# Gates issued among the tiles of a recurrent mixer's projection, a reordered beginning, and bias additions dealt out differently

## The reference, cut to what matters

```python
mod = (silu(c) @ w_ada + b_ada)                  # 6 x 1024 modulation values, from 12 panels of w_ada
h = rmsnorm(x, g_norm_mix) * (1 + sc1) + sh1
c_q, c_kv, k_pe, dil, gates = split(h @ w_in)    # projection
o_a = mla_attention(...)                         # 8 heads
o_g = dilated_band_attention(..., rel_bias, window, dilation)   # 3 groups x 8 heads
# scores there get a bias: bias_table[t5_bucket(rel)], 32 buckets, -1e30 outside the band
x = x + gt1 * ((g_a * o_a + g_b * o_b) @ w_out)
x = x + gt2 * expert_choice_ffn(h2, ...)         # 16 experts, 3 x 8 MB of weights each
```

```python
proj = u @ w_in + b_in                           # 1024 -> 2 x 1280: y half, then x half
ybr = gelu(proj[..., :1280])
xbr = causal_dwconv(proj[..., 1280:], conv_w, conv_b)    # 4 taps
gx = sigmoid(blockdiag(xbr, w_gx) + b_gx)        # 10 blocks of 128
ga = sigmoid(blockdiag(xbr, w_ga) + b_ga)
a = exp(8 * ga * log_sigmoid(lam))
b = sqrt(1 - a*a) * gx * xbr
h[t] = a[t] * h[t-1] + b[t]                      # scan over tokens
out = (h * ybr) @ w_out + b_out
```

## Time and profile before

| what | value |
|---|---|
| time, median of three runs | 2552.93 us (2550.88 to 2553.77) |
| the profiled execution's own time | 2551.12 us |
| its span, first to last instruction | 2549.3 us |
| TensorE busy | 86% of the span |
| VectorE, ScalarE busy | 36%, 14% |
| mean granted clock of TensorE | 0.931 of full |
| bytes read | 636 MB, 250 GB/s over the span |

### The profile page before, as it was taken

The page is one execution under the profiler, slowest core; times in us unless marked ns, Lnnn a source line. Parts: engine busy times, 40 slices in busy tenths (PEclk is TensorE's granted clock), DMA queues, the critical chain, the costliest instruction groups (busy, mean ns, idle before and its releaser), DMA issues.

```text
span 2549.3 us, 28377 instructions
## 1 busy us (share of the span) xinstructions
PE 2193.8 (86%) x11468; PEld 1540.3 (60%) x11468; DVE 916.1 (36%) x2034; ACT 363.1 (14%) x724; POOL 1.2 (0%) x16
## 2 busy tenths in 40 slices
PE   6999999997666666666666799999999998999999
PEld 4778888862222222222222288778888877788887
DVE  6796896131001100000100175626131336523233
ACT  2231111120000000000000022501010124101011
POOL 0000000000000000000000000000000000000000
PEclk9999999998888888878888899999999999999999
DMA  7526564469999999999999963044344431454420
GB/s 277 185 70 228 204 225 132 165 274 428 428 428 428 429 429 429 428 428 428 429 428 428 415 234 132 34 165 162 135 165 142 154 120 50 165 184 147 165 99 17
DMA packets 147476, 638.13 MB, mean 250 GB/s; under 512 B 10277, under 2 KB 52782, under 8 KB 119486
## 3 DMA queue, kind: packets, MB, share of 16 engines
q1 hardware_dynamic: 146446, 634.79, 63.4%
q10 hardware_dynamic: 944, 2.13, 0.2%
HBM read 635.86 MB, written 1.05 MB: 250 GB/s over the span
## 4 chain that ended last, share of the span: by engine, by line
PE 66%; DMA 27%; DVE 4%; ACT 2%; issue 1%; ACTq 0%; DVEq 0%; SPq 0%
DMA arena<-in_w_down_dram 19%; PE PS L1731 16%; PE PS L1131 13%; PE PS L1744 8%; PE PS L1044 7%; DMA arena<-in_w_up_dram 5%; DMA arena<-in_w_gate_dram 3%; PE PS L1498 3%; PE PS L1561 2%; PE PS L1517 2%; PE PS L1361 2%; DVE arena L1849 2%; PE PS L1695 2%; PE PS L1532 1%; PE PS L1489 1%; PE PS L1804 1%
## 5 line engine op out<-in xcount | busy, mean ns | idle before, releaser
L1498 PE MATMUL PS<-arena,hT 128*32 128x512 f32 x2048 | 304.2, 736 | 163.2 <-DMA arena<-in_w_up_dram 136.0
L1731 PE MATMUL PS<-arena 128*128 128x256 f32 x1920 | 416.7, 379 | 0.0
L1731 PEld LDWEIGHTS PS<-arena 128*128 128x128 f32 x1920 | 364.6, 190 | 49.8
L1498 PEld LDWEIGHTS PS<-arena,hT 128*32 128x32 f32 x2048 | 65.7, 124 | 383.5 <-DMA arena<-in_w_up_dram 212.6
L1131 PE MATMUL PS<-hT,arena 128*128 128x256 f32 (+1 forms) x1136 | 253.6, 383 | 1.5 <-ACT hT L717 1.5
L1517 PE MATMUL PS<-arena,hT 128*32 128x512 f32 x1008 | 171.5, 817 | 94.8 <-DMA arena<-in_w_down_dram 87.7
L1849 DVE SCALAR_TENSOR_TENSOR arena<-arena 128x512 f32<-128x512 f32 (+2 forms) x514 | 246.4, 547 | 0.8
L1131 PEld LDWEIGHTS PS<-hT,arena 128*128 128x128 f32 (+1 forms) x1136 | 213.3, 190 | 39.3 <-issue 9.7
L1846 DVE TENSOR_SCALAR arena<-arena,cols 128x256 f32<-128x256 f32 x162 | 66.3, 409 | 413.4 <-ACT arena L961 358.2
L1852 DVE TENSOR_TENSOR hT<-hT,PS 128x512 f32<-128x512 f32 x16 | 16.4, 1027 | 507.1 <-PE PS L1498 507.1
L1744 PE MATMUL PS<-arena 128*128 128x256 f32 x896 | 195.9, 379 | 0.0
(11 more groups left out here) (296 smaller groups left out, 1793.6 us busy)
## 6 DMA issues: line engine op xcount, KB each, us to landing
arena<-in_w_gate_dram SPq DMA_DIRECT2D x64, 2048.0 KB, 41.1
arena<-in_w_up_dram SPq DMA_DIRECT2D x64, 2048.0 KB, 40.9
arena<-in_w_down_dram SPq DMA_DIRECT2D x63, 2048.0 KB, 37.6
arena<-in_ffn_w_up_dram SPq DMA_DIRECT2D x32, 2048.0 KB, 8.5
arena<-in_w_in_dram SPq DMA_DIRECT2D x36, 1024.0 KB, 7.9
arena<-in_ffn_w_down_dram SPq DMA_DIRECT2D x16, 2048.0 KB, 7.9
arena<-in_w_ada_dram SPq DMA_DIRECT2D x12, 2048.0 KB, 11.7
arena<-in_ssd_w_in_dram SPq DMA_DIRECT2D x10, 2048.0 KB, 9.5
```

The costliest lines, as they stand in the source:

```text
L1498: mm = pe.matmul(PS[32 * f:32 * f + 32, 1 + half, :], xe[:, 32 * (2 * pi + k):32 * (2 * pi + k) + 32], w[:, k, 512 * f:512 * f + 512], sta ...
L1731: mm = pe.matmul(PS[:, n, T * half:T * half + T], slot(TAIL_SLOT[j], 8, 512)[:, k, P * n:P * n + P], hs[:, k, :], start=(k == 0), stop=(k ...
```

## The change

**Beginning.** `dmask` and `table` are fetched by SP's queue, after `mla_in` 0, and no longer by ScalarE's. TensorE no longer stops before `ada_rows(3)`: it waits for the far buckets after `proj(1)` and multiplies by `spread` after `proj(2)`. After `ada_rows(1)` and `ada_rows(2)` it runs four unused matmuls (`keep_busy(4)`). VectorE does four of the seven `near` steps before the modulation and the other three, the folding, the first one-hot and `far_bt` after its chunks of `hT`.

**Bias additions of heads 4 to 7.** Three before the loop; in q = 0 and q = 1 two between `max_part` and `norm_part`, six before `mix` and six after. `dil_turn(14)` moves behind the last projection tiles, `pt_copy(14)` behind the last copies.

**Recurrent mixer.** The x half comes first (tiles 0 to 9), then the y half. After each of tiles 9 to 13 TensorE issues two pairs of gates, into banks 4 to 7. Seven y tiles are taken out with Identity and get one Gelu of 128 x 1792 at the end; the last three get Gelu on the way out. Exp and Tanh run over all ten heads, then Sqrt over all ten. VectorE multiplies with y five heads later than it scans. Panel 2 of `lru_in` is fetched in two halves.

```diff
             load("mla_in", 0, at("mla_in", 0, 8, Q_RANK), w_in[:, :, 0:Q_RANK])
+            sp.dma_start(dmask.rearrange("p a b -> p (a b)"), A["dil_mask"]).then_inc(s["bias_in"], 16)
+            sp.dma_start(table, bass.AP(A["rel_bias"].tensor, 0, [[0, P], [1, BUCKETS * GROUPS * HEADS]])
+                         ).then_inc(s["bias_in"], 16)
...
             for j in range(4):
-                if j == 3:
-
-                    pe.wait_ge(s["near_ready"], 1)
-                    for c in range(TC):
-                        mm = pe.transpose(PS[0:16, 2, P * c:P * c + P], bucket[:, c, T + 64:KC], ident)
-                    mm.then_inc(s["far_t"], 1)
                 ada_rows(j)
-            pe.wait_ge(s["std_ready"], 1)
+                if j == 0:
+                    pe.wait_ge(s["std_ready"], 1)
+                if 1 <= j < 3:
+                    keep_busy(4)
             ada_turn(0)
...
-                if t == 0:
+                if t == 1:
+
+                    pe.wait_ge(s["near_ready"], 1)
...
+                if t == 2:
 
                     pe.wait_ge(s["far_bt"], 1)
...
-                    if i == (8 if q < 3 else 7):
+                    if i == 8:
                         dil_turn(a0)
...
+            bias_adds(3)
             for q in range(4):
                 a0 = 8 + 2 * q
                 max_part(a0)
                 max_part(a0 + 1)
+                bias_adds(2 if q < 2 else 0)
                 norm_part(a0)
                 norm_part(a0 + 1)
                 if q < 2:
-                    for n in range(step, step + 6):
-                        bias_add(n)
+                    bias_adds(6)
                     modulation(q + 1)
                 mix(a0)
                 mix(a0 + 1)
                 if q < 2:
-                    for n in range(step + 6, step + 16 - q):
-                        bias_add(n)
-                    step += 16
+                    bias_adds(6)
...
+            for m in range(4, 2 * NL):
+                j, n = m // 4, m % 4
...
+                if m >= 8:
+                    pe.wait_ge(s["ly_ready"], m - 3)
+                mm = tile(PS[:, n, 0:T], [(w[:, k, P * n:P * n + P], hs[:, k, :]) for k in range(KD)],
+                          norm=None if m > 4 else "mix_pre1")
...
+                if 0 <= m - FIRST_GATES < NL // 2:
+                    for h in (2 * (m - FIRST_GATES), 2 * (m - FIRST_GATES) + 1):
+                        lru_gate(h).then_inc(s["lg_gate_ps"], 1)
+            pe.wait_ge(s["lsig"], 2 * NL)
             open_rows()
...
+            for h in range(0, NL, 2):
+                gate_act(h)
+                gate_act(h + 1)
+                if h < NL - 2:
+                    y_tile(h // 2)
             act.wait_ge(s["lam_ready"], 3)
             act.wait_ge(s["lsig"], 2 * NL)
+            for h in range(NL):
+                act.activation(la[:, h, :], ga[:, h, :], ACT.Exp, scale=lam_c[:, h:h + 1]).then_inc(s["la_act"], 1)
+                act.activation(lt[:, h, :], ga[:, h, :], ACT.Tanh, scale=lam_d[:, h:h + 1]).then_inc(s["la_act"], 1)
+                if h in (4, 8, 9):
+                    y_tile((4, 8, 9).index(h) + 4)
+            for h in range(NL):
+                act.wait_ge(s["lb_chain"], 2 * h + 2)
+                act.activation(lt[:, h, :], lt[:, h, :], ACT.Sqrt).then_inc(s["lb_sqrt"], 1)
+            act.wait_ge(s["ly_ready"], NL + N_Y_GELU)
+            act.activation(yb[:, 0:N_Y_GELU, :], yb[:, 0:N_Y_GELU, :], ACT.Gelu_apprx_tanh).then_inc(s["ly_ready"], 1)
+            for t in range(N_Y_GELU, NL):
+                y_tile(t)
```

More of the change, by code:

```diff
@@ L45 @@
 NL = LRU_W // P
-LRU_GROUP = 5
 D_FF = 4096
@@ L101 @@
 LOOPED = ("ffn0", "ffn1")
+TWO_LOADS = (("lru_g", 0), ("lru_in", 2))
+FIRST_GATES, N_Y_GELU = 9, 7
 def early_stream():
@@ L817, in _ @@
                         exps(a0 + 1)
-                    if q == 3 and i == 16:
-                        pt_copy(a0)
+            pt_copy(14)
             pt_copy(15)
@@ L993, in _ @@
[L993 to L1001 removed]
+                act.activation(pads[:, t % 4, 3:3 + T], src, ACT.Identity, bias=cols[:, c:c + 1]
+                               ).then_inc(s["ly_ready"], 1)
@@ L1081, in _, with keep_busy @@
             square_sum("mix1", sq)
+            def keep_busy(n, bank=3):
+                for _ in range(n):
+                    pe.matmul(PS[:, bank, 0:T], ones, tri_ones, start=True, stop=True)
             def ada_rows(j):
@@ L1442, in token_turn @@
                 mm.then_inc(s["h2t_ps"], 1)
-            def keep_busy(n):
-                for _ in range(n):
-                    pe.matmul(PS[:, 3, 0:T], ones, tri_ones, start=True, stop=True)
             pe.wait_ge(s["std_ready"], NORM["ffn1"][0] + 1)
@@ L1905, in _, with near_step @@
             link(pc, stt(near, dist, 8.0, delta, ALU.min, ALU.add))
+            def near_step(start):
+                link(pc, stt(near, dist, float(start), near, ALU.is_ge, ALU.add))
             rms("mix1")
@@ L1910, in _ @@
                ALU.mult).then_inc(s["h_ready"], 1)
-            for start in BUCKET_STARTS:
-                link(pc, stt(near, dist, float(start), near, ALU.is_ge, ALU.add))
-            dve.memset(tiny[:, 118:119], 0.0).then_inc(s["pos_done"], 1)
-            dve.wait_ge(s["bias_in"], 112)
-            for c in range(TC):
-                for half in range(2):
-                    r = slice(64 * half, 64 * half + 64)
-                    dve.tensor_copy(bucket[r, c, T:T + 64], bucket[r, c, P * c + 64 * half:P * c + 64 * half + 64])
-                link(pc, stt(fold_tmp, dmask[:, c, T + P:512], 0.0, bucket[:, c, P * c:P * c + P], ALU.is_equal,
-                             ALU.mult))
-                link(pc, dve.tensor_reduce(bucket[:, c, T + 64:KC], fold_tmp.rearrange("p (b j) -> p j b", j=16),
-                                           AX.X, ALU.add))
             def bias_hot(n):
@@ L1972, in bias_fold @@
                 link("bias_fold", ins)
-            dve.memset(tiny[:, 119:120], 0.0).then_inc(s["near_ready"], 1)
-            bias_hot(0)
-            dve.wait_ge(s["far_t"], 1)
-            dve.tensor_copy(far_bucket, PS[0:16, 2, 0:T]).then_inc(s["far_bt"], 1)
+            for start in BUCKET_STARTS[:4]:
+                near_step(start)
             def modulation(g):
@@ L2000, in _ @@
                    ALU.add).then_inc(s["h1_dve"], 1)
+            for start in BUCKET_STARTS[4:]:
+                near_step(start)
+            dve.memset(tiny[:, 118:119], 0.0).then_inc(s["pos_done"], 1)
+            dve.wait_ge(s["bias_in"], 112)
+            for c in range(TC):
+                for half in range(2):
+                    r = slice(64 * half, 64 * half + 64)
+                    dve.tensor_copy(bucket[r, c, T:T + 64], bucket[r, c, P * c + 64 * half:P * c + 64 * half + 64])
+                link(pc, stt(fold_tmp, dmask[:, c, T + P:512], 0.0, bucket[:, c, P * c:P * c + P], ALU.is_equal,
+                             ALU.mult))
+                link(pc, dve.tensor_reduce(bucket[:, c, T + 64:KC], fold_tmp.rearrange("p (b j) -> p j b", j=16),
+                                           AX.X, ALU.add))
+            dve.memset(tiny[:, 119:120], 0.0).then_inc(s["near_ready"], 1)
+            bias_hot(0)
+            dve.wait_ge(s["far_t"], 1)
+            dve.tensor_copy(far_bucket, PS[0:16, 2, 0:T]).then_inc(s["far_bt"], 1)
             for i in range(2):
@@ L2092, in mix, with bias_adds @@
                    ).then_inc(s["mix_ready"], 1)
-            step = N_BUCKETS
+            later_bias = iter(range(N_BUCKETS, 2 * N_BUCKETS))
+            def bias_adds(count):
+                for n in itertools.islice(later_bias, count):
+                    bias_add(n)
+            bias_adds(3)
             for q in range(4):
```

122 lines of the change are left out of this document (60 added, 62 removed).

## The result

| | before | after |
|---|---|---|
| median, us (runs) | 2553.35 (4) | 2531.01 (4) |
| lowest and highest, us | 2550.88, 2553.89 | 2529.01, 2533.71 |
| span of the profiled execution, us | 2549.3 | 2527.2 |
| mean granted clock | 0.931 | 0.938 |

The ratio is 0.9917, with a 95% interval from 0.9902 to 0.9932. The forecast was 2530.8 us. The spans differ by 22.1 us, which is also the predicted sum; its terms are not all right, as will be seen.

What follows compares the result with a forecast made beforehand. Transfers were taken to bound the middle expert stage, which moves with what precedes it, and TensorE the rest. Gains of 4.5 + 6.2 + 11.4 = 22.1 us off 2552.93 gave 2530.8 us, range 2526 to 2540.

Steps and rivals of the forecast that it cites:

- Part 1: Beginning: panel 3 ends at 31.05 and not 36.08 us, less 0.5 for two transposes; 4.5 us gained, up to 6.3.
- I count no gain there: Beginning, `proj(0)`: idle time ahead stays, so its 5.25 us stay; 1.8 us for full pace kept for the range.
- the landing at 21.7: Beginning: panel 1 of `ada` lands at about 21.7 us, from which panel 3's landing at 29.3 was worked out.
- TensorE's own chain: Beginning: from 20.2 us, four panels and `keep_busy` at 1.7 each end at 28.8, so panel 3's transfer decides.
- rival B: VectorE's later bias work makes TensorE wait at first `mla_turn`, or late `table` holds `near_ready`; 2535.3 us, chance 0.17.
- Part 2: Bias additions: the 4.62 us wait at `dil_turn(12)` and 1.56 of slow stretch behind it go; 6.2 us gained.
- Part 3: Recurrent mixer: 9.5 us of wait before `lru_out` and 1.9 of slow start behind it go; 11.4 us gained.
- Rival C: Mixer: Identity copies cost table loads, making ScalarE the bound; `lru_out` 6.5 us late plus 1.9 slow; 2539.2 us, chance 0.12.
- Rival D: Beginning: `dmask` and `table` land late on SP's queue, delaying VectorE and then TensorE; 2558 us or more, chance 0.03.
- The sum: Whole kernel: gains of 4.5, 6.2 and 11.4 make 22.1 us, giving 2530.8 us; chance 0.62 that all pay.

Runs made afterwards that it cites:

- bias_only: Kernel before with only the bias additions dealt out anew and `dil_turn(14)` moved; 2546.89 us, ratio 0.9977.
- before_fill: Kernel before plus only unused matmuls: ahead of the first attention score, ahead of three `raw_tiles`, and in the router stage; 2543.65 us, ratio 0.9970.
- begin_only: Kernel before with only the edits of the beginning; 2549.77 us, ratio 0.9992, interval 0.9983-1.0001.
- gelu_each: Kernel after with Gelu at copy-out for each of the seven early y tiles, replacing Identity and the one late Gelu; 2541.77 us, ratio 0.9958.
- fill_all: Kernel after plus unused matmuls in four TensorE waits: ahead of the first attention score and of three `raw_tiles`; 2525.32 us, ratio 0.9896.
- after_again: Kernel after, unchanged, timed and profiled once more; 2529.97 us, ratio 0.9917 to the kernel before.
- late_gates: Kernel after with the gates behind tiles 14 to 18 and one Gelu over all ten y tiles; 2549.34 us, ratio 0.9990.
- best: Kernel after plus unused matmuls ahead of the first attention score, ahead of three `raw_tiles`, and in the router stage; 2526.68 us, ratio 0.9899.
- begin_fill: Kernel before with the new beginning plus unused matmuls ahead of the first score, three `raw_tiles` and in the router stage; 2542.68 us, ratio 0.9965.

## Why the prediction was right, step by step

- **Part 1**: 4.5 predicted, 6.03 measured in the pair of profiles. The step that missed there was "I count no gain there" for `proj(0)`: it ran at full pace, and 5.32 us became half of 7.14, 1.75 us less. Panel 3 ended at 31.50 (31.05 predicted), `proj(0)` began at 34.39 (34.0). Over all profiles, the first score is at 134.03, 133.11, 133.98 and 131.54 with the old beginning, mean 133.2, and at 128.7 in the mean of the eight that have the whole new one: 4.5 us. Executions of the same beginning differ by up to 2.6 us. Two other steps were not exact. The prediction lets TensorE wait for panel 1 inside the row at 20.19, but 32 instructions in 3.64 us are less than 2 x 1.92, so that row shows no wait; the landing at 21.7 is near the 22.04 and 21.86 at which bias_only and before_fill begin panel 1 after a wait. And TensorE's own chain was priced at 8.6 us, so that the transfer decides; it takes 9.3 (20.35 to 29.62 in begin_only). In four of the eight traces with the new beginning neither panel 2 nor 3 waits for its transfer, and TensorE reaches panel 3 at 29.6 to 30.3 by itself.
- **VectorE's lateness** (rival B) did not come. Its wait at the first rotation shrank from 6.86 to 2.03 us and stayed a wait.
- **Part 2**: 6.2 predicted, 6.34 measured, in the kernel after and in bias_only alike. The wait and the slow stretch behind it both went.
- **Part 3**: 9.5 + 1.9 predicted, 9.75 + 1.68 measured. ScalarE was ahead of the sum (the Gelu over 1792 columns done at 2133.3 where the sum had 2143.4 in old times, which is 2134.0 in the new ones); loads as forecast, one each.
- **Rival C**, made to happen in gelu_each, cost what it was priced at in the mixer (8.7 us, 8.4 priced). It failed in the kernel after since Identity needs no load between Sigmoid or Exp and Tanh.
- **Rival D** did not come: `dmask` and `table` were issued at 20.7 and 26.1 us, and VectorE's folding, which needs them, began at 37.25, right behind the three `near` steps, with no wait.
- **The sum** of 22.1 hit the 22.1 of the spans by an offset: the parts gave 23.8, and 1.7 went to differences of the clock in untouched stretches. The hit to 0.2 us by the medians is in part luck: the executions of the kernel after lie 4.7 us apart, and between the two kernels with filled waits the change measured 17.0 us. The prediction took everything outside the edited places as rigid. The expert stage moved with what lay ahead of it, as it said, but to within 3 us.

What stays open is what decides, in a given execution, behind which of the waits the clock falls. The waits ahead of the gather are equal in all kernels, apart from the wait of 1.71 us that three of them fill, and it was slow in ten of the fourteen profiles, in one of four executions of the same instructions. One thing holds in every trace here: `raw_tiles` behind 4.4 us of idle time are slow and behind 0.5 us are not. I did not run a version with part 1 taken out of the whole change, so its worth there (21.9 less 16.3 for the two other parts alone, 5.6 us) is worked out and not shown.

A version that measured faster than both kernels is fill_all: 26.2 us under the kernel before in its batch, where after_again was 21.9 under. The two did not run side by side, and their intervals (0.9881 to 0.9911, 0.9904 to 0.9931) overlap slightly.

## What to carry to other kernels

When a chain on another engine makes TensorE wait once near the end of a stage, look for the first operation of that chain that could be issued earlier among independent tiles: here the block with its gates five tiles earlier was 17 us shorter, and turning the halves round without that gained nothing. Price a removed wait together with the slow matmuls behind it, and fill waits like the norms' 4.4 us, which cannot be removed, with unused matmuls that end before what is waited for. A gain of 2 to 3 us from one part, measured alone in a program of this length, says little: compare at a place right behind the edit, and over several traces: in four traces of the same instructions the place 1455 us from the start moved by 4.8 us.

## What the runs showed of the hardware

- The granted clock falls at different places in executions of the same instructions: behind the same 1.80 us of wait 16 matmuls took 5.75 and 5.87 us in after and after_again and 3.72 in gelu_each and late_gates. Behind the same 0.28 and 0.47 us the gather and the first 128 instructions of expert 0 took 3.73 and 13.94 us in four profiles and up to 6.29 and 16.77 in the ten others.
- Nine unused matmuls ahead of a `raw_tiles` cut its 48 instructions to 10.60 us, in all four kernels that have them (fill_all, best, before_fill, begin_fill), from 12.0 to 13.6 us, without a later start: the 4.4 us of idle time ahead shrank to 0.5.
- Four unused matmuls behind each of two panels, 1.99 us each time, made the beginning 5.1 us shorter in one pair of profiles, and 2.5 us against the slowest trace with them, though they compute nothing.
- A table load costs 1.28 us and no drain in any of the 13 more of gelu_each, and the 8 in the gate loop did not delay TensorE: its last gate ends 43.2 us after the block's first tile in both kernels.
